# Pooling products in three reduced-precision passes, with the differences split into high and low parts by ScalarE and VectorE

## The chip, the core and the metric

The kernel runs on one core of a Trainium2 chip. The metric is the device time of one execution in microseconds (us), lower is better. The five engines of a core run side by side, each taking the instructions of its own queue in order: TensorE (PE: matmuls; its weight loads are PEld), VectorE (DVE), ScalarE (ACT), GpSimd (POOL) and SyncE (SP, here the issuer of most DMAs). They wait for each other through semaphores.

## What is computed

One decoder layer over a sequence of 1024 tokens of width 1024, all in float32. A normed input is projected to 1536 columns: 512 for a pooling mixer, 512 for a gated recurrence (RG-LRU), 512 for its gate. The mixers' outputs are normed, projected back and added, and a SwiGLU feed-forward layer follows. The change is in the pooling mixer:

```python
def pool_mixer(u, pool_w, pool_scale):
    for g, w in enumerate(POOL_WINDOWS):            # (2, 4, 8, 16)
        ug = uf[..., g * POOL_GROUP:(g + 1) * POOL_GROUP]
        cs = jnp.cumsum(ug, axis=1)
        lag = jnp.pad(cs[:, :S - w], ((0, 0), (w, 0), (0, 0)))
        mean = (cs - lag) / jnp.minimum(pos, float(w))
        outs.append(mean - ug)
    d = jnp.stack(outs, axis=2)
    y = jnp.einsum('bsgc,gcd->bsgd', d, pool_w.astype(jnp.float32)).reshape(B, S, POOL_WIDTH)
    return (y * pool_scale.astype(jnp.float32)).astype(u.dtype)
```

Each of the four groups has 128 channels and a 128x128 matrix, so a product here is 128x128 by 128x1024.

## The kernel before

Everything is held transposed, channels on the 128 partitions and tokens along the free dimension. Nearly all matmuls are done in three passes: an operand is split into a high part, rounded to the reduced-precision type fp32r by a ScalarE cast, and a low part, the rest, by a VectorE or GpSimd subtraction; then low x high, high x low and high x high are added up in one PSUM bank (`three_pass`, and `product` in the feed-forward layer). The gate matmuls of the recurrence (`gates`) and the pooling products (`pool_product`) are the exceptions: plain float32 matmuls on unsplit tiles.

The input projection runs over twelve blocks of 128 columns, c = 0 to 11. Blocks 0 to 3 feed the recurrence, 4 to 7 (from `POOL0` = 4) the pooling, 8 to 11 (from `GATE0` = 8) the gate. A block has two halves of 512 tokens, each 24 matmuls (8 row tiles x 3 passes). On every engine a loop over c writes out the order of the work by hand:
- TensorE: first half of block c; the gate matmuls of recurrence block c - 2 (c up to 5) or the pooling product p = c - 6 (c from 6 to 9, p = 0 to 3); second half; the other gate matmuls of c - 1. A product has two matmuls, one for each half of the tokens, into two banks that it shares with the gates.
- VectorE: in the round of block c it scales the first half out of PSUM (`first_half`, L1135), then does the recurrence c - 2 (`recur`, up to c = 5; ends with a scan, L1212), takes the result of product c - 6 out of PSUM with its gains (`pool_output`, L1240), makes the differences of the pooling block c - 4 (`window_mean`: p + 1 window sums L1224, the difference L1229, a repair of the first 16 tokens), and then the low part of the weights of block c + 2 (`split_w`, L1276), which TensorE needs in order to begin that block.
- ScalarE: in the round of block c it evacuates or activates the first half, takes the square root of the recurrence (L759), squares the product c - 6 (`pool_squares`, L771), evacuates the second half (L732, or the gelu L735), casts the weights of block c + 2 (`split_w`, L647) and does two sigmoids (L745).
- GpSimd adds the squares of products 1 to 3 to those of product 0 (L600).

The differences of product p lie in `xc[p % 2]`; `window_mean` may write them again once product p - 2 is done. `d_ok` counts the differences, `poolmm_ok` the halves of the products, `u_ok` and `u_first_ok` the evacuated halves, `w_lo_ok` the low parts of weights. In the last phase the blocks of the down weights (`dn`) have one semaphore each, for which ScalarE's `split_dn` and VectorE's `down_sum` wait.

Of the kernel before, what the change touches and what calls it, by code (L numbers as in the profile page):

```python
# [24 lines left out]
F32R = mybir.dt.float32r  # L25
ALU = mybir.AluOpType
ACT = mybir.ActivationFunctionType

P = 128
# [3 lines left out]
def hymba_pool_rglru_block(nc, x, ln1_g, w_in, pool_w, pool_scale, conv_w, conv_b, w_a, b_a, w_i, b_i,  # L33
                           lam, gn_pool_g, gn_lru_g, w_out, ln2_g, w_gate, w_up, w_down, lnf_g, out):
    S, D = x.shape[1], x.shape[2]
# [4 lines left out]
    GT = GW // P  # L40
# [4 lines left out]
    NP = FT // 2  # L45
# [8 lines left out]
    POOL0, GATE0 = GT, 2 * GT  # L54
# [10 lines left out]
    with ExitStack() as ctx:  # L65
# [3 lines left out]
        def at(name, kib, shape, dt=F32):  # L69
            return nc.alloc_sbuf_tensor_at(name, shape, dt, offset=BASE + int(kib * KIB))  # L70
# [9 lines left out]
        xc = [at(f"xc{s}", 120 + 4 * s, [P, S]) for s in range(2)]  # L80
# [21 lines left out]
        y1_lo = at("y1_lo", 168.25, [P, GT, S], F32R)  # L102
        sq_scr = at("sq_scr", 196.25, [P, 512])

        xs2 = [at(f"xs2_{s}", 116 - 4 * s, [P, D]) for s in range(2)]


# [79 lines left out]
        def sem(name):  # L187
            return ctx.enter_context(nc.semaphore(name))
# [7 lines left out]
        gate_1_in = sem("gate_1_in")  # L196
        hid_out = sem("hid_out")
        h_raw_in = [sem(f"h_raw_in{s}") for s in range(STEPS)]
        dn_in = {bk: sem(f"dn_in{bk[0]}_{bk[1]}") for bk in DN_ORDER}
        stored = sem("stored")  # L200

        consts = sem("consts")
# [15 lines left out]
        rb_ok = sem("rb_ok")  # L218
# [3 lines left out]
        sq_a_ok, sq_half_ok = sem("sq_a_ok"), sem("sq_half_ok")  # L222
        fin_act_ok = sem("fin_act_ok")
        psq_ok = sem("psq_ok")
        lsq_ok = sem("lsq_ok")
        ys_hi_ok, wo_hi_ok = sem("ys_hi_ok"), sem("wo_hi_ok")
        raw_ok = sem("raw_ok")
# [62 lines left out]
        def f32(ap):  # L290
            return ap.bitcast(F32)
# [4 lines left out]
        def half(i):  # L296
            return slice(i * HALF, (i + 1) * HALF)
# [344 lines left out]
        def _(act):  # L642
# [118 lines left out]
            def pool_squares(p):  # L761

                for i in range(2):
# [4 lines left out]
                    if p >= 2 and i == 0:  # L768
# [2 lines left out]
                    act.activation(dst[:, half(i)], pg[w % 2][:], ACT.Square, scale=v("pool_scale", p))\  # L771
                        .then_inc(psq_ok, 1)

            def lru_squares(g):
                act.wait_ge(lmul_ok, g + 1)
                if g >= 1:
                    act.wait_ge(ssum_ok, GT - 1 + g - 1)
                dst = ssum[1] if g == 0 else rg
                act.activation(dst[:], y[1][:, g, :], ACT.Square).then_inc(lsq_ok, 1)
# [37 lines left out]
            for c in range(2, NC_IN):  # L817
                if 0 <= c - 2 < GT:
                    sigmoids(c - 2, 1)
                    decay(c - 2)  # L820
                evacuate(c, 0)
                if 0 <= c - 2 < GT:
                    root(c - 2)
                if 0 <= c - POOL0 - 2 < GT:
                    pool_squares(c - POOL0 - 2)
                if c == NC_IN - 1:
                    y_hi_part(0)
                    y_hi_part(1)
                    group_sqrt(0)
                evacuate(c, 1)  # L830
                if c + 2 < NC_IN:
                    split_w(c + 2)
                if 0 <= c - 1 < GT:
                    sigmoids(c - 1, 0)
                if c - 1 >= GATE0:
                    lru_squares(c - 1 - GATE0)
                if c == NC_IN - 2:
                    split_wo(0)
# [138 lines left out]
            def split_dn(s):  # L977
                i, k = s // NP, s % NP
                pr = PRODUCTS[i]
                if pr in ("M1", "M2", "M3"):  # L980
                    act.wait_ge(dn_in[D_BLOCK[pr], k], 16)
                else:
                    act.wait_ge(dsum_ok, dsum_count(DSUM_OF[pr], k))
                if s < STEPS:
                    act.wait_ge(ent_ok, done(entry(FT - 1, "M6")) if s < EARLY else NE)
                act.copy(d_hi[s % STEPS][:], dn[D_BLOCK[pr], k][:]).then_inc(d_hi_ok, 1)
# [87 lines left out]
        def _(dve):  # L1074
# [139 lines left out]
            def window_mean(p):  # L1214
# [18 lines left out]
                                              op0=ALU.max, op1=ALU.mult))  # L1233
                dve.tensor_tensor(d[:, 0:PAD], dfix[:], src[:, PAD:2 * PAD], ALU.subtract).then_inc(d_ok, 1)

            def pool_output(p):
                for i in range(2):
                    w = 2 * p + i
                    dve.wait_ge(psq_ok, w + 1)
                    dve.tensor_scalar(y[0][:, p, half(i)], pg[w % 2][:], v("pool_scale", p), v("gn_pool", p),  # L1240
                                      ALU.mult, ALU.mult).then_inc(pool_y, 1)
# [36 lines left out]
            for c in range(NC_IN):  # L1278
                if c >= 2:
                    first_half(c)  # L1280
                if 0 <= c - 2 < GT:
                    recur(c - 2)
                if 0 <= c - POOL0 - 2 < GT:
                    pool_output(c - POOL0 - 2)
                if c < POOL0:
                    convolve(c)
                    if c == 0:
                        softplus()
                elif c < GATE0:
                    window_mean(c - POOL0)  # L1290
                else:
                    if c == NC_IN - 1:
                        group_variance(0)
                        group_rsqrt(0)
                    gate_lru(c - GATE0)
                    if c > GATE0:
                        lru_gain(c - GATE0 - 1)
                if c + 2 < NC_IN:
                    split_w(c + 2)
                if c == NC_IN - 2:  # L1300
                    split_wo(0)
# [194 lines left out]
            def down_sum(name, k):  # L1496
                b11, b12, b21, b22 = (dn[b, k][:] for b in ("11", "12", "21", "22"))
                if name == "T3":
                    dve.wait_ge(dn_in["22", k], 16)
                    dve.wait_ge(dn_in["12", k], 16)  # L1500
                    dve.tensor_tensor(b12, b22, b12, ALU.subtract).then_inc(dsum_ok, 1)
                if name == "T2":
                    dve.wait_ge(d_lo_ok, k + 1)
                    dve.wait_ge(dsum_ok, dsum_count("T3", k))
                    dve.tensor_tensor(b11, b12, b11, ALU.add).then_inc(dsum_ok, 1)
                if name == "T1":
                    dve.wait_ge(d_lo_ok, 3 * NP + k + 1)
                    dve.wait_ge(dsum_ok, dsum_count("T2", k))
                    dve.tensor_tensor(b12, b22, b11, ALU.subtract).then_inc(dsum_ok, 1)
                if name == "T4":  # L1510
                    dve.wait_ge(dn_in["21", k], 16)
                    dve.wait_ge(dsum_ok, dsum_count("T1", k))
                    dve.tensor_tensor(b11, b21, b11, ALU.subtract).then_inc(dsum_ok, 1)
# [87 lines left out]
        def _(pe):  # L1601
# [53 lines left out]
                        .then_inc(gates_ok, 1)  # L1655

            def pool_product(p):
                pe.wait_ge(d_ok, p + 1)
                for i in range(2):
                    w = 2 * p + i  # L1660
                    if p == 0:
                        pe.wait_ge(gate_evac, 4 * GT - 1 + i)
                    else:
                        pe.wait_ge(pool_y, w - 1)
                    pe.matmul(pg[w % 2][:], pool_ws[:, p], xc[p % 2][:, half(i)], start=True, stop=True)\  # L1665
                        .then_inc(poolmm_ok, 1)

            def group_sums(g):

# [206 lines left out]
```

## Time and profile before

| | before |
|---|---|
| median of three runs | 922.02 us (921.94 to 923.41) |
| the profiled execution: time, span | 922.02 us, 920.2 us |
| busy share of TensorE, VectorE, ScalarE, GpSimd | 97%, 66%, 42%, 30% |
| chain of work that ended last | TensorE 95%, VectorE 3%, DMA 1% |
| pooling products (L1665) | 16 records of 592 ns |
| a load of one block of input weights, 512 KB | 3.7 us from issue to landing |

The span is the time from the first to the last instruction of the profiled execution; the time of a run has some 1.8 us more around it. A float32 matmul leaves two records in the trace, a pass of a split one leaves one. Matmuls are pipelined: a record of 0.39 us overlaps the next, so the cost of one is the distance between the starts. The granted clock tells at which of its two levels (2.4 GHz: 1.00; 1.2 GHz: 0.5) TensorE ran. In a timeline row stand the start, the duration, the engine and line, the operation, what it writes and reads, its shape and the count of merged instructions, and in brackets how long the engine had idled and for whom.

### The profile page before, as it was taken

The numbers are of one execution on the slowest core, as the hardware profiler recorded it, in microseconds if no ns is written. First come the engines' busy times: TensorE is split into PE (matmuls) and PEld (weight loads), VectorE is DVE, ScalarE is ACT, GpSimd is POOL, SyncE is SP. The second block draws the span as 40 slices with busy tenths as digits, with TensorE's granted clock in tenths as the row PEclk, the third lists the DMA queues.
The fourth block names the chain that finished last, engine by engine and source line by source line (L and its number), as shares of the span: only waits on it lengthen the run. The fifth ranks groups of instructions, "written<-read, shape, count | busy, mean of one in ns | idle before, by whom it ended". The sixth has DMA issues, their size and how long they took to land.

```text
span 920.2 us, 10969 instructions
## 1 busy us (share of the span) xinstructions
PE 895.2 (97%) x3955; PEld 731.2 (79%) x3955; DVE 606.0 (66%) x836; ACT 388.4 (42%) x645; POOL 277.6 (30%) x213
## 2 busy tenths in 40 slices
PE   5989999999999999999999999999999999999996
PEld 4757777888888788888888888888888888888885
DVE  5568885455568866565665656646566985687766
ACT  5668723433466433322323233232334343445455
POOL 3000012255043755446455545555551000000000
PEclk9999999999999999999999999999999999999998
DMA  9010110204002132233322423324238943332324
GB/s 320 1 47 23 46 46 24 92 1 159 24 1 70 46 125 81 92 126 92 126 95 78 149 70 125 109 71 154 72 111 307 405 145 103 92 103 93 98 86 183
DMA packets 93790, 96.43 MB, mean 105 GB/s; under 512 B 5628, under 2 KB 63528, under 8 KB 93736
## 3 DMA queue, kind: packets, MB, share of 16 engines
q1 hardware_dynamic: 83224, 76.32, 24.5%
q10 hardware_dynamic: 10512, 19.40, 6.8%
q8 instruction: 32, 0.52, 0.2%
q14 instruction: 22, 0.18, 0.1%
HBM read 71.33 MB, written 24.38 MB: 104 GB/s over the span
## 4 chain that ended last, share of the span: by engine, by line
PE 95%; DVE 3%; DMA 1%; issue 1%; ACT 0%; POOL 0%; DVEq 0%; ACTq 0%
PE bank L1734 23%; PE bank L1736 23%; PE bank L1735 23%; PE bank L1606 8%; PE bank L1608 7%; PE bank L1607 7%; PE bank L1623 1%; PE bank L1654 1%; PE bank L1665 1%; DVE nT_lo L1127 1%; DMA g_row<-in_ln_g 1%; DVE xc L1118 0%; PE bank L1672 0%; DVE xc L1193 0%; DVE xc L1120 0%
## 5 line engine op out<-in xcount | busy, mean ns | idle before, releaser
L618 POOL TENSOR_TENSOR r_lo<-gu_raw,r_hi 128x512 fp32r<-128x512 f32 x84 | 116.4, 1385 | 68.1 <-ACT r_hi L862 68.0
L618 POOL TENSOR_TENSOR r_lo<-wsum_S,r_hi 128x512 fp32r<-128x512 f32 x63 | 98.7, 1567 | 125.7 <-ACT r_hi L862 125.7
L1734 PE MATMUL bank<-T_hi,r_lo 128*128 128x512 f32 x336 | 130.9, 390 | 0.9 <-DVE u L1461 0.9
L1736 PE MATMUL bank<-T_hi,r_hi 128*128 128x512 f32 x336 | 130.7, 389 | 0.0
L1735 PE MATMUL bank<-T_lo,r_hi 128*128 128x512 f32 x336 | 130.7, 389 | 0.0
L1734 PE MATMUL bank<-d_hi,h_lo 128*128 128x512 f32 x308 | 119.8, 389 | 0.0
L1735 PE MATMUL bank<-d_lo,h_hi 128*128 128x512 f32 x308 | 119.8, 389 | 0.0
L1736 PE MATMUL bank<-d_hi,h_hi 128*128 128x512 f32 x308 | 119.8, 389 | 0.0
L862 ACT CAST r_hi<-gu_raw 128x512 fp32r<-128x512 f32 x84 | 52.2, 621 | 131.4 <-PE bank L1736 131.4
L1734 PE MATMUL bank<-nT_hi,r_lo 128*128 128x512 f32 x252 | 98.1, 389 | 0.0
L1735 PE MATMUL bank<-nT_lo,r_hi 128*128 128x512 f32 x252 | 98.0, 389 | 0.0
L1736 PE MATMUL bank<-nT_hi,r_hi 128*128 128x512 f32 x252 | 98.0, 389 | 0.0
L975 ACT CAST h_hi<-h_raw 128x512 fp32r<-128x512 f32 x76 | 47.2, 622 | 102.5 <-PE bank L1736 98.0
L1606 PE MATMUL bank<-nT_hi,w_lo 128*128 128x512 f32 x192 | 81.2, 423 | 5.1 <-DVE nT_lo L1127 2.6
L1439 DVE TENSOR_TENSOR h_lo<-h_raw,h_hi 128x512 fp32r<-128x512 f32 x76 | 52.5, 691 | 47.8 <-ACT h_hi L975 47.8
L1608 PE MATMUL bank<-nT_hi,w_hi 128*128 128x512 f32 x192 | 75.5, 393 | 0.0
L1607 PE MATMUL bank<-nT_lo,w_hi 128*128 128x512 f32 x192 | 75.5, 393 | 0.0
L1734 PEld LDWEIGHTS bank<-T_hi,r_lo 128*128 128x128 f32 x336 | 63.1, 188 | 14.6 <-POOL r_lo L618 1.3
L1736 PEld LDWEIGHTS bank<-T_hi,r_hi 128*128 128x128 f32 x336 | 63.1, 188 | 13.2
L1735 PEld LDWEIGHTS bank<-T_lo,r_hi 128*128 128x128 f32 x336 | 63.1, 188 | 13.1
L1734 PEld LDWEIGHTS bank<-d_hi,h_lo 128*128 128x128 f32 x308 | 57.8, 188 | 12.1
L1735 PEld LDWEIGHTS bank<-d_lo,h_hi 128*128 128x128 f32 x308 | 57.8, 188 | 12.0
(208 smaller groups left out, 1627.1 us busy)
## 6 DMA issues: line engine op xcount, KB each, us to landing
h_raw<-hid_ops ACTq DMA_DIRECT2D x72, 256.0 KB, 2.6
gu_raw<-in_w_ffn_gate SPq DMA_DIRECT2D x22, 512.0 KB, 3.7
gu_raw<-in_w_ffn_up SPq DMA_DIRECT2D x22, 512.0 KB, 4.7
hid_ops<-hid SPq DMA_DIRECT2D x44, 256.0 KB, 2.2
dn<-in_w_ffn_down SPq DMA_DIRECT2D x44, 256.0 KB, 10.8
hid_ops<-hsum_S SPq DMA_DIRECT2D x33, 256.0 KB, 2.5
w_raw<-in_w_in SPq DMA_DIRECT2D x12, 512.0 KB, 3.7
h<-in_x SPq DMA_DIRECT2D x8, 512.0 KB, 7.6
```

Of the source, the lines that this page charges most:

```text
L618: pool.tensor_tensor(lo_of(n)[:], a_block(f, name), f32(hi_of(n)[:]), ALU.subtract)\
L862: act.copy(hi_of(n)[:], a_block(f, name)).then_inc(r_hi_ok, 1)
L975: act.copy(h_hi[s % STEPS][:], h_source(s)[:]).then_inc(h_hi_ok, 1)
L1127: dve.tensor_tensor(nT_lo[dst], pt_of(n)[b][:].rearrange("p (k n) -> p k n", k=4), f32(nT_hi[dst]), ALU.subtract).then_inc(n_lo_ok, 1)
L1439: dve.tensor_tensor(h_lo[s % STEPS][:], h_source(s)[:], f32(h_hi[s % STEPS][:]), ALU.subtract)\
L1606: pe.matmul(bank, s_lo, m_hi, start=(k == 0), stop=False)
L1607: pe.matmul(bank, s_hi, m_lo, start=False, stop=False)
L1608: ins = pe.matmul(bank, s_hi, m_hi, start=False, stop=(k == n - 1))
L1623: ins = pe.transpose(pt_of(n)[b][:, cols(k)], xs[n % 2][:, cols(4 * b + k)], ident[:])
L1734: pe.matmul(bank, s_lo, m_hi, start=(opens and j == 0), stop=False, skip_group_check=True)
L1735: pe.matmul(bank, s_hi, m_lo, start=False, stop=False, skip_group_check=True)
L1736: ins = pe.matmul(bank, s_hi, m_hi, start=False, stop=(closes and j == n - 1), skip_group_check=True)
```

## The change

Each pooling product becomes six fp32r matmuls instead of two float32 ones. The weights are split once: ScalarE casts all four matrices at the end of the round of block 4 (`pool_weights_hi`), VectorE subtracts in the round of block 5 (`pool_weights_lo`, in place). The differences of product p are split in the round of block p + 5: ScalarE casts them behind the squares and ahead of the second half's evacuation (`pool_hi`), VectorE subtracts in place ahead of the next block's window sums (`pool_lo`). The product waits for the low parts. The high parts lie in space that is free at that time, which adds two waits to ScalarE (for the last scan, and for product p - 2). In the last phase the blocks "12" and "22" of the down weights share a semaphore, since both are loaded in turn.

```diff
+        pw_hi, pw_lo = at("pw_hi", 200.5, [P, GT, P], F32R), at("pw_lo", 188.25, [P, GT, P], F32R)
+        pd_hi = [at(f"pd_hi{s}", (164.25, 148.25)[s], [P, S], F32R) for s in range(2)]
+        pd_lo = [at(f"pd_lo{s}", 120 + 4 * s, [P, S], F32R) for s in range(2)]
...
-        dn_in = {bk: sem(f"dn_in{bk[0]}_{bk[1]}") for bk in DN_ORDER}
+        dn_in = {bk: sem(f"dn_in{bk[0]}_{bk[1]}") for bk in DN_ORDER if bk[0] != "12"}
+        for k in range(NP):
+            dn_in["12", k] = dn_in["22", k]
...
+            def pool_weights_hi():
+                act.wait_ge(small_in, 16 * 5)
+                act.wait_ge(rb_ok, 1)
+                act.copy(pw_hi[:], pool_ws[:]).then_inc(pw_hi_ok, 1)
+            def pool_hi(p):
+                act.wait_ge(d_ok, p + 1)
+                if p == 1:
+                    act.wait_ge(scan_ok, GT)
+                if p >= 2:
+                    act.wait_ge(poolmm_ok, 2 * (p - 1))
+                act.copy(pd_hi[p % 2][:], xc[p % 2][:]).then_inc(pd_hi_ok, 1)
...
                 if 0 <= c - POOL0 - 2 < GT:
                     pool_squares(c - POOL0 - 2)
+                if 0 <= c - POOL0 - 1 < GT:
+                    pool_hi(c - POOL0 - 1)
...
                 evacuate(c, 1)
+                if c == POOL0:
+                    pool_weights_hi()
...
-                    act.wait_ge(dn_in[D_BLOCK[pr], k], 16)
+                    act.wait_ge(dn_in[D_BLOCK[pr], k], 32 if pr == "M3" else 16)
...
+            def pool_weights_lo():
+                dve.wait_ge(pw_hi_ok, 1)
+                dve.tensor_tensor(pw_lo[:], pool_ws[:], f32(pw_hi[:]), ALU.subtract).then_inc(pw_lo_ok, 1)
+            def pool_lo(p):
+                dve.wait_ge(pd_hi_ok, p + 1)
+                dve.tensor_tensor(pd_lo[p % 2][:], xc[p % 2][:], f32(pd_hi[p % 2][:]), ALU.subtract).then_inc(pd_lo_ok, 1)
...
                 if 0 <= c - POOL0 - 2 < GT:
                     pool_output(c - POOL0 - 2)
+                if c == POOL0 + 1:
+                    pool_weights_lo()
+                if 0 <= c - POOL0 - 1 < GT:
+                    pool_lo(c - POOL0 - 1)
                 if c < POOL0:
                     convolve(c)
...
-                    dve.wait_ge(dn_in["22", k], 16)
-                    dve.wait_ge(dn_in["12", k], 16)
+                    dve.wait_ge(dn_in["22", k], 32)
...
             def pool_product(p):
-                pe.wait_ge(d_ok, p + 1)
+                pe.wait_ge(pw_lo_ok, 1)
+                pe.wait_ge(pd_lo_ok, p + 1)
                 for i in range(2):
                     w = 2 * p + i
...
-                    pe.matmul(pg[w % 2][:], pool_ws[:, p], xc[p % 2][:, half(i)], start=True, stop=True)\
-                        .then_inc(poolmm_ok, 1)
+                    three_pass(pg[w % 2][:], [(pw_hi[:, p], pw_lo[:, p], pd_hi[p % 2][:, half(i)],
+                                               pd_lo[p % 2][:, half(i)])]).then_inc(poolmm_ok, 1)
```

## Rows read from the trace of the kernel before

**Rows 1.** Windows view, 100 to 180 us: busy time (instructions) of each engine, clock, DMA
```profile
100.00:180.00 80.00, 80.00 (x343) 62.97 (x342) 54.50 (x56) 29.41 (x39) 10.17 (x5) 1.00 0.14 43
```

**Rows 2.** Waits of TensorE: total us, times, longest
```profile
PE bank L1606 <- DVE w_lo L1276: 2.5, 1, 2.5
...
PE bank L1606 <- POOL y_lo L625: 0.5, 1, 0.5
```

**Rows 3.** Timeline of TensorE, 101 to 153 us: start, us, instruction, [idle before]
```profile
101.85 1.88 PE L1654 MATMUL bank<-xc,gate_w 128*128 128x512 f32 x4
...
109.05 0.39 PE L1606 MATMUL bank<-nT_hi,w_lo 128*128 128x512 f32 x1
...
114.49 1.88 PE L1665 MATMUL bank<-xc,pool_ws 128*128 128x512 f32 x4
...
127.14 1.88 PE L1665 MATMUL bank<-xc,pool_ws 128*128 128x512 f32 x4
...
152.43 1.88 PE L1665 MATMUL bank<-xc,pool_ws 128*128 128x512 f32 x4
```

**Rows 4.** Timeline of VectorE, 115 to 124 us
```profile
115.23 1.20 DVE L1224 TENSOR_TENSOR sumA<-ub 128x1024 f32<-128x1024 f32 x1
...
119.28 1.22 DVE L1276 TENSOR_TENSOR w_lo<-w_raw,w_hi 128x1024 fp32r<-128x1024 f32 x1
...
121.99 1.53 DVE L1240 TENSOR_SCALAR y<-bank,vec 128x512 f32<-128x512 f32 x2 [0.88 <-ACT ig L771]
123.43 1.21 DVE L1224 TENSOR_TENSOR sumA<-ub 128x1024 f32<-128x1024 f32 x1
```

**Rows 5.** One line's instructions: VectorE split of 128x512, ns min/median/max
```profile
L1439 DVE TENSOR_TENSOR h_lo<-h_raw,h_hi x76: 682/692/695, 698.8 to 900.2; 128x512 fp32r<-128x512 f32 x76
```

**Rows 6.** Instruction groups by line: ScalarE cast of 128x1024, 80 to 330 us
```profile
L647 ACT CAST w_hi<-w_raw 128x1024 fp32r<-128x1024 f32 x7 | 7.4, 1052 | 0.0
```

**Rows 7.** Timeline of ScalarE, 99 to 123 us
```profile
99.97 0.68 ACT L745 ACTIVATE ig<-bank,vec 128x512 f32<-128x512 f32 x1
...
110.38 0.57 ACT L732 COPY ub<-bank 128x512 f32<-128x512 f32 x1
...
121.26 1.27 ACT L771 ACTIVATE ig<-bank,vec 128x512 f32<-128x512 f32 x2 [9.37 <-DVE ub L1135]
122.42 0.59 ACT L732 COPY ub<-bank 128x512 f32<-128x512 f32 x1
```

**Rows 8.** Timeline of VectorE, 128 to 143 us
```profile
128.76 1.22 DVE L1276 TENSOR_TENSOR w_lo<-w_raw,w_hi 128x1024 fp32r<-128x1024 f32 x1
...
135.23 1.23 DVE L1224 TENSOR_TENSOR sumA<-ub 128x1024 f32<-128x1024 f32 x1 [2.23 <-ACT ub L732]
...
141.83 1.22 DVE L1276 TENSOR_TENSOR w_lo<-w_raw,w_hi 128x1024 fp32r<-128x1024 f32 x1
142.97 0.68 DVE L1135 TENSOR_TENSOR ub<-bank,rb 128x512 f32<-128x512 f32 x1
```

**Rows 9.** Timeline of ScalarE, 143 to 146 us
```profile
143.75 1.28 ACT L735 ACT_TABLE_LOAD   x1 [7.67 <-DVE ub L1135]
...
145.58 1.25 ACT L771 ACTIVATE rg<-bank,vec 128x512 f32<-128x512 f32 x2
```

**Rows 10.** Timeline, GpSimd's second addition of squares
```profile
146.91 2.41 POOL L600 TENSOR_TENSOR ig<-ig,rg 128x1024 f32<-128x1024 f32 x1 [12.42 <-ACT rg L771]
```

**Rows 11.** Timeline of VectorE, beside that addition
```profile
147.82 2.58 DVE L1246 TENSOR_TENSOR y<-y,ub 128x1024 f32<-128x1024 f32 x1
```

**Rows 12.** Timeline of VectorE, the low weights that it waited for
```profile
51.56 1.22 DVE L1276 TENSOR_TENSOR w_lo<-w_raw,w_hi 128x1024 fp32r<-128x1024 f32 x1
```

**Rows 13.** Timeline of TensorE, its one wait for low weights
```profile
52.83 0.50 PE L1606 MATMUL bank<-nT_hi,w_lo 128*128 128x512 f32 x1 [2.48 <-DVE w_lo L1276]
```

**Rows 14.** Windows view, two early stretches; the clock is the number behind GpSimd's
```profile
14.00:21.00 7.00, 4.41 (x14) 3.37 (x13) 5.05 (x13) 6.50 (x12) 3.75 (x2) 0.76 1.10 367
...
48.00:53.00 5.00, 2.15 (x5) 0.85 (x6) 4.45 (x21) 4.57 (x6) 0.00 (x0) 1.00 0.01 2
```

More of the change, by code:

```diff
@@ L224, in hymba_pool_rglru_block @@
         psq_ok = sem("psq_ok")
+        pw_hi_ok, pw_lo_ok, pd_hi_ok, pd_lo_ok = (sem(n) for n in ("pw_hi_ok", "pw_lo_ok", "pd_hi_ok", "pd_lo_ok"))
         lsq_ok = sem("lsq_ok")
```

## The prediction

> **What bounds the kernel now.** I read the windows view first. From 100 to 180 us, the stretch that holds all four pooling products, TensorE is busy for the whole of it at a granted clock of 1.00 (its 2.4 GHz level), VectorE for 54.5 us of 80, ScalarE for 29.4 [rows 1]. Then TensorE's waits: it waits once for a low part of weights, for 2.5 us before this stretch, and once behind it, 0.5 us, for a low part that GpSimd makes [rows 2]. So TensorE sets the time. What it no longer has to do is won one for one, and what it must newly wait for is lost one for one. Both VectorE and ScalarE are half idle on average, but an average doesn't say whether a part is ready at the moment when TensorE asks; for that the timelines have to be laid side by side.
>
> **What the products cost on TensorE.** I number the column blocks c = 0 to 11; blocks 4 to 7 are the pooling ones, and product p (0 to 3) stands inside block p + 6, between its two halves. Each half of a block is 24 matmuls. The first half of block 6 starts at 109.05 and product 0 at 114.49, so 24 matmuls take 5.44 us, 0.2267 each [rows 3]. From product 0 to product 1 are 12.65 us (product 3 lies two such periods further on, to 0.01); less 48 x 0.2267 = 10.88, a full-precision product of four records costs 1.77 us [rows 3]. In three passes it is 2 halves x 3 = 6 matmuls of the kind around it: 6 x 0.2267 = 1.36. The gain is 0.41 each and 4 x 0.41 = 1.64 in all. The period between products falls from 12.65 to 12.24.
>
> **What it costs elsewhere: product 0.** Until now product 0 needed only the differences, and these are made in VectorE's round of block 4. The low half of them is made in the round of block 5, and there VectorE runs the last recurrence first: what follows its scan, today the first window sum, starts at 115.23 [rows 4]. That alone is 0.74 us after TensorE reaches product 0. Now two splits come ahead of the window sum. The weights' low part is 128x512 elements, 0.69 us [rows 5], less 0.08 of overlap with the next instruction (two back-to-back instructions start 1.14 apart where the first takes 1.22 [rows 8]), so 0.61; the other split can start at 115.84. The differences' low part is 128x1024, as the split of weights beside it, 1.22 us [rows 4]: done at 117.06. ScalarE's high part is ready: its round of block 5 is free at 110.38 [rows 7], a cast takes 1.05 [rows 6], so about 111.4. TensorE starts a matmul 0.05 after a low part lands (51.56 + 1.22 to 52.83), and the first one after a wait lasts 0.50 instead of 0.39 [rows 3, 12, 13]. Product 0 therefore starts at 117.11 instead of 114.49, and the stall is 2.62 + 0.11 = 2.73 us. Nothing covers it, since TensorE takes its queue in order and the second half of block 6 is behind it.
>
> **The other edits, followed down the chain.** TensorE's products now stand at 117.22 (with the 0.11), and then every 12.24: 129.46, 141.70, 153.94. VectorE's chain is what must keep up.
> - Block 6. The two splits move VectorE's work by 0.61 + 1.14 = 1.75. The weights' low part of block 7, today 119.28 to 120.50 [rows 4], ends at 122.25; TensorE wants it at 117.22 + 1.36 + 5.44 = 124.02. Covered, but only because of the stall: without one it would be wanted at 121.29. The first half's scaling runs 1.14 behind the start of the split, from 122.17 to 122.85; ScalarE's squares follow 0.16 later, at 123.01 (121.10 to 121.26 today), with 1.16 to its next instruction [rows 7], and the cast runs from 124.17 to 125.22. VectorE's low part of product 1 runs from 125.30 to 126.52 and the window sums start at 126.44, against 123.43 [rows 4]: a shift of 3.01. Product 1 asks at 129.46, covered by 2.9.
> - Block 7. With the shift of 3.01 the low weights of block 8 end at 132.99 [rows 8]; wanted at 136.26. By the same steps the scaling ends at 133.59, the squares of product 1 run from 133.75 to 135.02, and GpSimd adds them to the sum from 135.10 for 2.4 us. ScalarE's cast ends at 135.96, so VectorE's low part of product 2 comes while GpSimd adds. The trace has this meeting once: GpSimd's addition from 146.91 to 149.32 and a VectorE product of two tiles from 147.82, which lasts 2.58 instead of 1.23 and ends 1.08 after GpSimd [rows 10, 11]. I take that: the low part ends at 137.50 + 1.08 = 138.58, and the window sums start at 138.50 against 135.23, a shift of 3.27 [rows 8]. The 2.23 us that VectorE idled there are used up. Product 2 asks at 141.70, covered by 3.1. The low weights of block 9 end at 146.32; wanted at 148.50.
> - Block 8. The scaling ends at 142.97 + 3.27 + 0.68 = 146.92 [rows 8]. From there a table load, the gelu and the squares take ScalarE to 146.92 + 0.10 + 3.08 = 150.10 (143.75 to 146.83 today [rows 9]), and the last cast to about 151.05. GpSimd adds from 150.18 to 152.58, so the last low part ends at 153.66, with 0.05 for TensorE 153.71. Product 3 asks at 153.94: covered by 0.23 only. Behind it come a gate product and the low weights of block 10, 1.2 each, done by about 156.1 and wanted at 153.94 + 1.36 + 5.44 = 160.74.
> - Queued behind ScalarE's casts are the second half's evacuation and the next weights' high part. In block 5 the evacuation moves from 110.38 to about 111.4 [rows 7], read by the window sums after 117; in the others the low part, which waits for the same cast, is later anyway. The load of block 9's weights on SP's queue waits for the low part at 122.25, 1.75 later than today, takes 3.7 us (the table) and is read by ScalarE after 135.
> - The weights' high part, a ScalarE cast of half the size and so at most 1.05 [rows 6], delays the sigmoids whose last one ends at 100.65 [rows 7] and which release the gate matmuls that start at 101.85 [rows 3]. It is hidden, as I put it at about half of 1.05; if it cost all of it, still within 1.2. The one semaphore for two blocks of the down weights counts the same two transfers; its waits end where the later one ended. Nothing.
>
> A rule of the page "SBUF — State Buffer" of the Trainium skill ("Who interferes with whom") says the same of the block: a VectorE instruction with two SBUF inputs and a GpSimd one that reads SBUF exclude each other for the whole instruction, whoever came first. The trace agrees (2.58 against 1.23). If they only shared, each of the two low parts would last about 1.3 us less and product 3 would have some 2.9 to spare; the sum stays, since product 0 is stalled before GpSimd adds anything.
>
> **The sum.** -1.64 + 2.73 = +1.09 us. The profiled execution has a span of 920.2 and a time of 922.02, which is also the median; 1.8 lie around the span. All that follows block 9 hangs on TensorE (the 0.5 for GpSimd's low part too: its chain starts at the last block's gelu), so the 1.09 arrive at the end: 923.1 us. The sum is robust downward: if product 0 were late by less, TensorE would reach block 7 and product 3 earlier and wait there, for 122.25 and 153.71, which are VectorE's times. By VectorE's chain alone the three last steps would still give 153.71 + 0.11 - 152.43 - 0.41 = +0.98. Upward there is no such floor: each delay of VectorE's chain beyond 0.23 us arrives at product 3.
>
> **Rivals.**
> 1. Slower: the last high part comes late. In block 8 ScalarE goes from gelu to squares to the cast and back to gelu. If the cast between them cost one more table load, 1.28 [rows 9], ahead of it, the last low part would be ready at 154.99 and product 3 would stall for 1.05 + 0.11: 923.1 + 1.16 = 924.3, slower by 0.24%. It decides from 0.23 us on, and passes the bound from 0.9. Against it: today a cast of weights stands between such gelus, and VectorE's longer idle times have no load in them. For it: the cover is a quarter of a microsecond at the end of a chain of some twenty instructions. 0.19.
> 2. No stall: product 0 finds its low part ready and the gain stands alone, 922.02 - 1.64 = 920.4. For this the split would have to be over by 114.49, but the recurrence ahead of it isn't. 0.04. A gain of more than 0.2% has no cause in the rows beyond this one.
> 3. Three passes bring nothing, because switching from and to full precision costs less than I count or weight loads come in between: +2.73, 924.8. Against it stand hundreds of such matmuls at 0.2267 with loads beside them. 0.03.
> 4. The pause costs TensorE its clock. Today it stood for 2.48 us and the granted clock stayed 1.00 [rows 13, 14]; early on, with TensorE busy for 4.4 of 7 us, it was 0.76 over them, so 0.24 x 7 = 1.7 us lost at most [rows 14]. 923.1 + 1.7 = 924.8. 0.04.
> Of this the page "TensorE: Matmul & The Clock Gate" ("What's actually happening") says that the array is throttled by default and activity releases it; the trace shows one pause of the same length without a drop, so I go by the trace.
>
> **How the numbers follow.** Forecast 0.70, with a range of its own of 922.4 to 923.8 (0.7 either way for the twenty-odd durations and the spread of the three runs of before, 921.94 to 923.41). A measurement of this kernel tells about 0.2%, 1.84 us, from no change: 920.18 and 923.86. Slower: rivals 1, 3 and 4, 0.26, of which some fall under the bound: 0.24. Faster: 0.03, from rival 2. Same: 0.73. The range reaches up to rival 1 and down past my own range: 921.6 to 924.6.
>
> **What would show it.** In the changed kernel TensorE waits for the differences' low part once, for about 2.6 us, at product 0, and for nothing at block 7; products are some 12.24 apart; VectorE's low parts 2 and 3 last about 2.5 us instead of 1.22; product 3 follows within 0.3 us of its low part. The forecast is wrong if product 0 doesn't wait, if product 3 waits for over 0.5, or if TensorE's clock falls after product 0.

## Result and the profile after

| | before | after |
|---|---|---|
| median | 922.1 us (17 runs, 921.94 to 924.76) | 924.64 us (17 runs, 923.08 to 926.16) |
| ratio after / before | | 1.0021, 95% interval 1.0014 to 1.0028 |
| the profiled execution: span | 920.2 us | 924.3 us |
| TensorE, VectorE, ScalarE, GpSimd busy, us | 895.2, 606.0, 388.4, 277.6 | 897.7, 612.7, 392.6, 276.9 |

The changed kernel is slower by about 2 us where 1.09 was forecast. The measured median lies 0.04 above the top of the range that was given (924.6); by the ratio, 922.02 x 1.0021 = 924.0 lies inside, and above the forecast's own range (923.8). It is on the far side of the prediction's 0.2% line, if only just: "slower" had 0.24, "same" 0.73. The seventeen runs don't scatter about one value. Four lie at 923.08 to 923.13, six at 924.49 to 924.81, and seven at 925.06 to 926.16. The first group is the forecast (922.02 + 1.09 = 923.11) and the question is what the others pay.

The profiled execution is one of the longest (926.14 us). Its timeline of TensorE at product 0 (start, us, instruction, idle before) answers to the product in [rows 3]:

```profile
115.63 0.39 PE L1647 MATMUL bank<-nT_hi,w_hi 128*128 128x512 f32 x1
118.51 0.56 PE L1645 MATMUL bank<-pd_hi,pw_lo 128*128 128x512 f32 x1 [2.49 <-issue]
118.87 0.63 PE L1646 MATMUL bank<-pd_lo,pw_hi 128*128 128x512 f32 x1
119.29 0.63 PE L1647 MATMUL bank<-pd_hi,pw_hi 128*128 128x512 f32 x1
...
121.43 0.63 PE L1646 MATMUL bank<-nT_lo,w_hi 128*128 128x512 f32 x1
121.85 0.54 PE L1647 MATMUL bank<-nT_hi,w_hi 128*128 128x512 f32 x1
122.23 0.40 PE L1645 MATMUL bank<-nT_hi,w_lo 128*128 128x512 f32 x1
```

The pause is there, 2.49 us idle (the view names "issue" because the wait stands ahead of the product and not on the matmul). Behind it the matmuls are 0.427 us apart instead of 0.2267, until 122.23: nine of them and the start take 3.72 us where 9 x 0.2267 + 0.11 = 2.15 would do. That is 1.57 us on top of the pause. The windows view (us, then busy time of TensorE, its weight loads, VectorE, ScalarE, GpSimd; the number behind GpSimd's is the granted clock), first after, then before:

```profile
14.00:21.00 7.00, 4.42 (x15) 3.40 (x14) 5.05 (x13) 6.54 (x12) 3.77 (x2) 0.76 1.09 363
54.00:58.00 4.00, 4.00 (x13) 3.10 (x12) 3.47 (x3) 0.00 (x0) 0.00 (x0) 0.59 0.40 118
118.00:122.00 4.00, 3.49 (x9) 2.74 (x10) 3.93 (x4) 0.00 (x0) 0.00 (x0) 0.59 0.00 0
```

```profile
54.00:58.00 4.00, 4.00 (x20) 3.28 (x19) 3.71 (x3) 0.00 (x0) 0.00 (x0) 1.00 0.45 130
118.00:122.00 4.00, 4.00 (x19) 3.29 (x19) 3.05 (x6) 0.74 (x2) 0.00 (x0) 1.00 0.03 8
```

Apart from the start, where both kernels show 0.76, TensorE's clock fell to its 1.2 GHz level twice in this execution of the changed kernel: at product 0, and near 54 us, behind the older pause for the low weights of block 2, in code that the change doesn't touch. In the profiled execution of before it fell at neither, though the older pause was there [rows 13].

### The profile page after: what moved, and what is told of

It reads as the page before. It is cut to its first block, busy times and chain, and to the rows that moved or that the text cites. A ratio compares the mean times of both kernels' runs of the same rounds, so it can differ in the third digit from the quotient of the medians.

```text
span 924.3 us, 10988 instructions
## 1 busy us (share of the span) xinstructions
PE 897.7 (97%) x3963; PEld 735.5 (80%) x3963; DVE 612.7 (66%) x841; ACT 392.6 (42%) x650; POOL 276.9 (30%) x213
## 4 chain that ended last, share of the span: by engine, by line
PE 89%; DVE 6%; issue 2%; ACT 2%; DMA 1%; POOL 0%; ACTq 0%; DVEq 0%
PE bank L1774 23%; PE bank L1776 23%; PE bank L1775 23%; PE bank L1645 6%; PE bank L1647 6%; PE bank L1646 6%; PE bank L1662 1%; DVE xc L1221 1%; DVE nT_lo L1155 1%; DMA g_row<-in_ln_g 1%; DVE t2b L1236 1%; DVE w_lo L1312 1%; ACT t2b L768 0%; DVE xc L1146 0%; ACT L768 0%
## 5 line engine op out<-in xcount | busy, mean ns | idle before, releaser
L1776 PEld LDWEIGHTS bank<-d_hi,h_hi 128*128 128x128 f32 x308 | 57.8, 188 | 12.1
```

The source lines that it names most:

```text
L1776: ins = pe.matmul(bank, s_hi, m_hi, start=False, stop=(closes and j == n - 1), skip_group_check=True)
```

## The experiments

Theory A: the sum of the prediction holds (+1.09), and the rest is the clock that falls in the pause at product 0 in many executions (rival 4, which had 0.04). Theory B: the rest is somewhere else, in product 3 waiting for its low part (rival 1) or in another part of the change. Each kernel below ran in five rounds beside the kernel before; "mean" below is against the mean of all 108 runs of the kernel before that stood beside the changed kernel or the experiments, 922.83 (lowest 921.85).

**The changed kernel again.**

> The changed kernel unaltered, beside the next three on one chip. All theories: its runs lie at 923.1 or above, median about 924.6. Theory A: none lies between 922.2 and 923.0, and those above 923.1 are 1.2 to 3.2 us higher, by one or two falls of the clock (start, 50 us, product 0).

Ratio 1.0022 (1.0013 to 1.0031), median 924.6; two of 11 runs at 923.13 and 923.18, none below. This time the profiled execution is one of the lowest (923.18, span 921.4), with the clock at 1.00 from 54 to 58 and from 118 to 122. It shows the change without any fall. TensorE at the four products, and then VectorE's splits and low weights:

```profile
117.13 0.47 PE L1645 MATMUL bank<-pd_hi,pw_lo 128*128 128x512 f32 x1 [2.48 <-issue]
...
129.49 0.39 PE L1645 MATMUL bank<-pd_hi,pw_lo 128*128 128x512 f32 x1
...
141.73 0.39 PE L1645 MATMUL bank<-pd_hi,pw_lo 128*128 128x512 f32 x1
...
153.97 0.39 PE L1645 MATMUL bank<-pd_hi,pw_lo 128*128 128x512 f32 x1
```

```profile
115.23 0.67 DVE L1266 TENSOR_TENSOR pw_lo<-pool_ws,pw_hi 128x512 fp32r<-128x512 f32 x1
115.81 1.22 DVE L1270 TENSOR_TENSOR pd_lo<-xc,pd_hi 128x1024 fp32r<-128x1024 f32 x1
...
121.02 1.22 DVE L1312 TENSOR_TENSOR w_lo<-w_raw,w_hi 128x1024 fp32r<-128x1024 f32 x1
...
125.24 1.22 DVE L1270 TENSOR_TENSOR pd_lo<-xc,pd_hi 128x1024 fp32r<-128x1024 f32 x1
...
135.94 2.60 DVE L1270 TENSOR_TENSOR pd_lo<-xc,pd_hi 128x1024 fp32r<-128x1024 f32 x1
...
145.05 1.22 DVE L1312 TENSOR_TENSOR w_lo<-w_raw,w_hi 128x1024 fp32r<-128x1024 f32 x1
...
151.02 2.61 DVE L1270 TENSOR_TENSOR pd_lo<-xc,pd_hi 128x1024 fp32r<-128x1024 f32 x1
```

The prediction had the products at 117.11, 129.46, 141.70 and 153.94. Product 3's low part ends at 151.02 + 2.61 = 153.63; with 0.05 for the start it is covered by 0.29 (0.23 was said). Low parts 2 and 3 last 2.6 us because GpSimd adds squares from 135.06 and 150.13:

```profile
135.06 2.40 POOL L609 TENSOR_TENSOR ig<-ig,rg 128x1024 f32<-128x1024 f32 x1 [116.38 <-ACT rg L780]
150.13 2.42 POOL L609 TENSOR_TENSOR ig<-ig,rg 128x1024 f32<-128x1024 f32 x1 [12.67 <-ACT rg L780]
```

135.06 + 2.40 = 137.46, and the low part ends 1.08 later, as in [rows 10, 11]. So rival 1 did not happen.

This profile also prices the change without the start of the kernel, which differs from execution to execution. I measure from the first matmul of block 2, behind the older pause, to the last store that is issued ("SPq" is SP's queue); first the changed kernel's two rows, then the last one of before, whose first is in [rows 13]:

```profile
52.85 0.50 PE L1645 MATMUL bank<-nT_hi,w_lo 128*128 128x512 f32 x1 [2.47 <-DVE w_lo L1312]
...
918.72 0.43 SPq L570 DMA_DIRECT2D out_dram<-h  x1
```

```profile
917.58 0.43 SPq L561 DMA_DIRECT2D out_dram<-h  x1
```

918.72 - 52.85 = 865.87 against 917.58 - 52.83 = 864.75: +1.12 us, where the sum was +1.09. And it accounts for the execution of 926.14 us. That one takes 1.64 us more from block 2's first matmul to product 0 (65.92 against 64.28, the fall near 54 us) and 1.57 more from product 0 to the last store (803.16 against 801.59, the fall at product 0). Nothing is left for a third cause.

**The pause filled.** TensorE does idle matmuls (their result is read by nobody) while it waits at product 0:

```diff
             def pool_product(p):
+                if p == 0:
+                    for _ in range(10):
+                        pe.matmul(pt[0][:], nT_hi[:, 0, 0:P], nT_hi[:, 1, half(0)], start=True, stop=True)
                 pe.wait_ge(pw_lo_ok, 1)
```

> The changed kernel with ten idle matmuls (of normed input tiles, into a bank that nobody reads) ahead of product 0's wait: 10 x 0.2267 = 2.27 us of the 2.6 us for which TensorE stands still there. Theory A (the pause lets TensorE's clock fall to its 1.2 GHz level, which costs about 1.4 us on top of the wait): the clock stays at 1.00 through 118 to 122 us, product 0 starts when it did, and the median falls from about 924.6 to 923.1 to 923.5, what is left over 923.1 coming from the older pause near 50 us. Theory B (the excess over the forecast comes from product 3 waiting for its low part, or from the last phase): nothing changes, about 924.6.

```profile
117.05 2.43 PE L1699 MATMUL bank<-nT_hi 128*128 128x512 f32 x10
119.70 0.47 PE L1645 MATMUL bank<-pd_hi,pw_lo 128*128 128x512 f32 x1 [0.22 <-issue]
```

```profile
54.00:58.00 4.00, 4.00 (x11) 3.21 (x12) 3.93 (x4) 0.00 (x0) 0.00 (x0) 0.62 0.46 131
118.00:122.00 4.00, 3.78 (x17) 2.85 (x16) 3.96 (x4) 0.00 (x0) 0.00 (x0) 1.00 0.00 0
```

Median 923.57, ratio 1.0013 (1.0004 to 1.0022), mean +1.13 where the changed kernel's 28 runs have +1.97. Five of 11 runs lie at 923.06 to 923.21. The product starts as late as before (VectorE's chain stands where it stood, the execution being 2.6 us late by falls at the start and at 54 us), but the clock behind the pause is 1.00. The median is 0.07 above the expected range. The means differ by 1.97 - 1.13 = 0.84 us, which would be 1.57 in about every second execution. This figure is rough: single runs of a kernel differ by up to 3 us, the two ratios' intervals overlap, and on 11 and 28 runs I estimate the 0.84 to about 0.7 either way. That the mean comes within 0.04 of the sum, 1.09, is luck, since it holds falls elsewhere too, as the mean of before does. A second estimate comes from the lowest group: 6 of the changed kernel's 28 runs lie in it (up to 923.2) and 44 of the 108 of before (up to 922.1). If the falls are independent of each other, the one at product 0 spares about half of the executions. The profiled run, 925.73, owes its length to falls elsewhere; that the other one above 925.7 does too is inferred.

**Three-pass products alone**, of tiles that are there already. The splits are left out on ScalarE and VectorE, and the products are of other data, so this kernel doesn't compute the layer; it only times the products:

```diff
             def pool_product(p):
-                pe.wait_ge(pw_lo_ok, 1)
-                pe.wait_ge(pd_lo_ok, p + 1)
+                pe.wait_ge(d_ok, p + 1)
...
-                    three_pass(pg[w % 2][:], [(pw_hi[:, p], pw_lo[:, p], pd_hi[p % 2][:, half(i)],
-                                               pd_lo[p % 2][:, half(i)])]).then_inc(poolmm_ok, 1)
+                    three_pass(pg[w % 2][:], [(nT_hi[:, p, 0:P], nT_hi[:, p, 0:P], nT_hi[:, p, half(i)],
+                                               nT_lo[:, p, half(i)])]).then_inc(poolmm_ok, 1)
```

> Three-pass products alone: six fp32r matmuls for each product, but of normed input tiles that are there already, with no splits and with the wait for the differences as before the change. The splits of weights and differences are left out and the products are of other data. Both theories: no pause at product 0, the products 12.24 us apart, 0.41 x 4 = 1.64 us less than the kernel before, 920.4 (ratio 0.9982). A rival that the three passes save nothing: 922.0.

Lowest runs 920.28 to 920.32 (five of 11), against 921.85 to 922.07 before; mean -1.56, ratio 0.9984 (0.9975 to 0.9993). The first two products in the profile:

```profile
117.02 0.39 PE L1637 MATMUL bank<-nT_hi 128*128 128x512 f32 x1
...
129.26 0.39 PE L1637 MATMUL bank<-nT_hi 128*128 128x512 f32 x1
```

They are 12.24 us apart, and there is no pause. The gain term of 4 x 0.41 is right; rival 3 falls.

**Splits and waits alone**, the products in full precision and the low parts in space of their own: once as it is, and once with idle matmuls in both pauses (the ten at product 0, nine ahead of block 2).

```diff
...
-        pd_lo = [at(f"pd_lo{s}", 120 + 4 * s, [P, S], F32R) for s in range(2)]
+        pd_lo = [at(f"pd_lo{p}", 164.25 if p == 3 else 160.25, [P, S], F32R) for p in range(4)]
...
-                    three_pass(pg[w % 2][:], [(pw_hi[:, p], pw_lo[:, p], pd_hi[p % 2][:, half(i)],
-                                               pd_lo[p % 2][:, half(i)])]).then_inc(poolmm_ok, 1)
+                    pe.matmul(pg[w % 2][:], pool_ws[:, p], xc[p % 2][:, half(i)], start=True, stop=True)\
+                        .then_inc(poolmm_ok, 1)
```

> The splits and the waits alone: everything of the change but the products, which stay in full precision and read the unsplit tiles; the low parts are written aside. A pause of 2.6 us at product 0 and nothing won: by the sum +2.73, 924.8 without a fall of the clock. Theory A: with the fall, some 1.4 more in most runs, median about 926.2. Theory B: 924.8.

> The splits and waits with full-precision products, with the idle matmuls in both pauses. The pause at product 0 priced by itself without the clock: 922.0 + 2.73 = 924.8, or 923.7 where the start-up runs without its fall; median 924.8, against 926.9 without the idle matmuls. If splits and waits cost something besides the pause and the clock, it stays above 925.5.

Without the idle matmuls: median 926.93 of only five runs, mean +4.03; none at 924.8. With them: median 924.76, mean +2.12, five of ten runs at 924.4 to 924.8, four at 925.5 to 925.7 and one at 923.73. From block 2's first matmul to the last store the profiled execution with them takes 867.45 us, +2.70 against before: that is the 2.73 of the prediction. The means of the two kernels differ by 1.9 us, and all five runs without idle matmuls are longer than all ten with them; since both pauses are filled at once, this doesn't say which of the two falls it saves. The profile without them shows that a pause alone decides nothing. The clock had fallen at the start and near 54 us; at product 0 TensorE stood idle as long as in the changed kernel, and the clock stayed:

```profile
116.70 0.39 PE L1649 MATMUL bank<-nT_hi,w_hi 128*128 128x512 f32 x1
119.57 1.96 PE L1707 MATMUL bank<-xc,pool_ws 128*128 128x512 f32 x4 [2.49 <-issue]
...
120.96 0.79 PE L1647 MATMUL bank<-nT_hi,w_lo 128*128 128x512 f32 x1
```

```profile
118.00:122.00 4.00, 2.43 (x7) 1.42 (x8) 3.93 (x5) 0.00 (x0) 0.00 (x0) 1.00 0.00 0
```

(From the product to the next matmul of a block are 1.39 us; in the kernel before, without a pause, 1.32, from 114.49 to 115.81.) The same 2.49 us of pause cost 1.57 us in one execution and nothing in another.

**The kernel before, with its own pause filled.**

```diff
                 u = position(c, i)
+                if i == 0 and c == 2:
+                    for _ in range(9):
+                        pe.matmul(pt[0][:], nT_hi[:, 0, 0:P], nT_hi[:, 1, half(0)], start=True, stop=True)
                 if i == 0:
                     pe.wait_ge(w_lo_ok, c + 1)
```

> The kernel before with nine idle matmuls ahead of its wait for the low weights of block 2 (2.5 us near 50 us). Theory A, applied to the older pause: the runs of the kernel before that take 923.4 instead of 922.0 are those in which the clock falls there; with the idle matmuls all runs take 922.0, and the highest stays under 922.6. Theory B: the spread of 1.4 us stays.

Ten of 11 runs lie between 920.92 and 922.04, the last at 923.13, against a highest of 924.70 and a median of 923.1 for the kernel before beside it. Ratio 0.9989 (0.998 to 0.9998). So the spread of the kernel before is for the most part the same thing: a pause in which the clock falls or not. "All runs at 922.0" was wrong in both directions.

There is a third place, the start of the kernel. In the windows view from 14 to 21 us the granted clock was 0.76 to 0.78 in nine of the fourteen profiles, 0.63 to 0.65 in four, and 1.00 in one (a run of 920.47 of a kernel below). One of the four (a run of 921.45 of the last kernel below, whose median is 920.35), and the one with 1.00, with its next 7 us:

```profile
14.00:21.00 7.00, 4.41 (x13) 3.33 (x12) 5.05 (x13) 6.51 (x12) 3.77 (x2) 0.63 1.10 368
```

```profile
14.00:21.00 7.00, 4.41 (x21) 3.53 (x20) 5.05 (x13) 6.53 (x12) 3.78 (x2) 1.00 1.10 365
21.00:28.00 7.00, 5.13 (x27) 4.28 (x26) 5.11 (x11) 3.38 (x8) 0.00 (x0) 0.83 0.21 63
```

In the second the low stretch isn't missing; it comes later. What each start costs shows at the first matmul of block 2: 52.48 us with the late stretch, 52.59 to 52.92 with 0.76 to 0.78, and 53.91 to 54.03 in the four with 0.63 to 0.65. So the longer low stretch costs about 1.1 us, which fits a run at 923.1. Runs 1.1 us *below* the usual lowest ones, as 920.9 here, are in no profile. Their mean granted clock on record is 0.998 against 0.994 to 0.997 of this kernel's others, so it is the clock; but they appear only with idle matmuls ahead of block 2 (8 of the 53 runs of the five kernels that have them, none of the 108 of before), and why that is stays open.

**Both pauses filled in the changed kernel.**

> The changed kernel with idle matmuls in both pauses: nine ahead of block 2, ten ahead of product 0. Theory A (the sum +1.09 stands, and the rest of the excess is TensorE's clock falling in pauses): the clock stays at 1.00 in both places in the profile, nothing lies above 924.3, and the median is 923.1 or, where the start-up too runs without its fall (1.1 less, as in the lowest runs with the matmuls ahead of block 2), 922.0 to 923.1. A rest of theory B (an excess that has nothing to do with pauses): median over 924.

Ratio 1.0008 (1.0000 to 1.0017), median 923.18, the profiled execution 923.09 with the clock at 1.00 in both places. Five of 11 runs at 923.00 to 923.18, one at 922.20, but five at 924.0 to 924.45, one of which is above the 924.3 that was said. They lie 1.1 above the group at 923.1, as a longer low stretch at the start would put them. Their mean granted clock is 0.993 to 0.995, that of the group at 923.1 0.996 to 0.997, so it is the clock; no profile of one of them was taken, so where it fell stays open. In the profiled execution block 2's first matmul to the last store takes 865.85 us, +1.10 against 864.75, both in before and in before with its own pause filled. The runs of these two kernels with filled pauses differ by 1.26 in the median and 1.73 in the mean: the profile gives the sum, and the mean holds more falls than the pauses that were filled.

**Product 0 left in full precision**, products 1 to 3 as in the change (their waits and the weights' splits are counted without product 0):

```diff
-                if 0 <= c - POOL0 - 1 < GT:
+                if 1 <= c - POOL0 - 1 < GT:
                     pool_hi(c - POOL0 - 1)
...
-                if 0 <= c - POOL0 - 1 < GT:
+                if 1 <= c - POOL0 - 1 < GT:
                     pool_lo(c - POOL0 - 1)
...
+                    if p == 0:
+                        pe.matmul(pg[w % 2][:], pool_ws[:, 0], xc[0][:, half(i)], start=True, stop=True)\
+                            .then_inc(poolmm_ok, 1)
+                        continue
```

> The changed kernel with product 0 left in full precision on the unsplit tiles; products 1 to 3 in three passes. No split and no wait for product 0. From the rows of before: three gains of 0.41; product 3 would be asked for at 152.43 - 2 x 0.41 = 151.61, while VectorE's low part is ready at about 152.5, 1.1 to 1.2 earlier than in the change because one split fewer stands ahead of it: a pause of 0.9 + 0.11. Sum -1.23 + 1.0 = -0.2, lowest runs 921.8. Theory A: a pause of 0.9 does not bring the clock down, so the distribution is that of the kernel before, shifted by -0.2 (ratio 0.9998). If VectorE's chain doesn't matter at product 3: -1.2, 920.8.

Lowest runs 921.72 and 921.75, 0.3 below 922.02 where 0.2 was said; mean -0.03, ratio 0.9997 (0.9988 to 1.0006). Product 3 now waits, and its distance to product 2 is 13.09 instead of 12.24, a pause of 0.85 (0.9 + 0.11 was said):

```profile
141.10 0.39 PE L1645 MATMUL bank<-pd_hi,pw_lo 128*128 128x512 f32 x1
...
154.19 0.47 PE L1645 MATMUL bank<-pd_hi,pw_lo 128*128 128x512 f32 x1 [0.69 <-issue]
```

This is the kind of floor of which the prediction spoke: without the pause at product 0 VectorE's chain holds up product 3 instead, and most of the gain of three products, 0.85 of 1.23, goes there. Its 11 runs span 921.7 to 924.4, as the kernel before's span 921.9 to 924.65: this shorter pause brings no new group of runs.

**The splits moved, so that no product waits.** Product 0 in full precision; then, in a second kernel, all four in three passes. The calls stand at their new places only.

```diff
                     decay(c - 2)
+                if 1 <= c - POOL0 - 1 < GT:
+                    pool_hi(c - POOL0 - 1)
                 evacuate(c, 0)
...
                 if c >= 2:
                     first_half(c)
+                if c == POOL0 + 1:
+                    pool_weights_lo()
+                if 1 <= c - POOL0 - 1 < GT:
+                    pool_lo(c - POOL0 - 1)
```

> Product 0 in full precision as before, products 1 to 3 in three passes, and the splits moved: ScalarE's cast at the top of its round, where it idles for 6 to 10 us waiting for VectorE's first scaling; VectorE's low part right behind that scaling, where it overlaps the squares and ends before GpSimd's addition starts; the weights' low part ahead of the last recurrence. No low part is late and none meets GpSimd: each lasts 1.22. All theories: -3 x 0.41 = -1.23, lowest runs 920.8, ratio 0.9987. If the moved splits delay anything (a second half's evacuation, the low weights of blocks 8 and 9), up to 0.5 of it is lost.

> The same with the nine idle matmuls ahead of the wait for the low weights of block 2. Theory A: same lowest runs (920.8) but fewer above them, as in the kernel before with these matmuls; median 920.8, ratio to the kernel before about 0.998.

The second kernel begins `pool_hi` with product 0 and has besides:

```diff
+                if j == GT - 1:
+                    pool_lo(0)
                 dve.wait_ge(sqrt_ok, j + 1)
...
+                    if c == POOL0 + 1:
+                        split_w(c + 2)
                     window_mean(c - POOL0)
...
-                if c + 2 < NC_IN:
+                if c + 2 < NC_IN and c != POOL0 + 1:
                     split_w(c + 2)
```

> All four products in three passes, none late: the high part of product 0 is cast between ScalarE's exponential and its square root, its low part taken in the 2.5 us in which VectorE waits for that root, the weights' low part ahead of the recurrence, the low weights of block 7 ahead of the window sums of the second pooling block; products 1 to 3 as in the kernel with the splits moved. The last recurrence ends 1.0 us later. -4 x 0.41 = -1.64: lowest runs 920.4, ratio to the kernel before 0.998. Rival: the recurrence's 1.0 us comes out at the low weights of block 7 or 8, and it is no faster than the kernel with product 0 in full precision, 920.8.

> The same with the nine idle matmuls ahead of block 2. Lowest runs 919.3 (start-up without its fall) or 920.4, median 920.2 to 920.4, ratio to the kernel before 0.9975: the fastest of all kernels here.

| kernel | median, us | lowest | ratio to before (95%) |
|---|---|---|---|
| product 0 full, splits moved | 920.86 | 920.81 | 0.9986 (0.9976 to 0.9995) |
| the same, idle matmuls ahead of block 2 | 920.68 | 919.75 | 0.9979 (0.9970 to 0.9988) |
| all four split, splits moved | 920.46 | 920.24 | 0.9985 (0.9976 to 0.9994) |
| the same, idle matmuls ahead of block 2 | 920.35 | 919.38 | 0.9974 (0.9965 to 0.9984) |

All beat both kernels. Seven of the first one's 11 runs lie at 920.81 to 920.87, where 922.02 - 1.23 = 920.79 was the sum. With all four split the low part of product 0 lies in VectorE's idle time and the low parts of the later ones last 1.22 us again, since they come ahead of GpSimd's addition. In the timeline of VectorE of that kernel the first of them waits 0.5 us for ScalarE's cast and is still done 4 us before the product:

```profile
108.87 1.23 DVE L1272 TENSOR_TENSOR pd_lo<-xc,pd_hi 128x1024 fp32r<-128x1024 f32 x1 [0.47 <-ACT pd_hi L796]
...
132.00 1.21 DVE L1272 TENSOR_TENSOR pd_lo<-xc,pd_hi 128x1024 fp32r<-128x1024 f32 x1
...
144.19 1.22 DVE L1272 TENSOR_TENSOR pd_lo<-xc,pd_hi 128x1024 fp32r<-128x1024 f32 x1
```

```profile
114.29 0.39 PE L1649 MATMUL bank<-pd_hi,pw_lo 128*128 128x512 f32 x1
```

Whether the fourth product's 0.41 is really there can't be told from the ratios (their intervals overlap). From the profiles it can. The table has, from the first matmul of block 2 to the last store, every profiled execution whose clock stayed at 1.00 in between, up to the last matmul:

| kernel | us | against before |
|---|---|---|
| before; before, pause filled | 864.75; 864.75 | 0 |
| changed; changed, both pauses filled | 865.87; 865.85 | +1.12; +1.10 |
| splits and waits alone, both filled | 867.45 | +2.70 |
| product 0 full, splits moved; with idle matmuls | 863.56; 863.51 | -1.19; -1.24 |
| all four split, splits moved; with idle matmuls | 863.11; 863.09 | -1.64; -1.66 |

The fourth product brings 0.42 to 0.45. The terms of the prediction's sum come out to 0.04 us in single executions, where the ratios' intervals are over 1 us wide.

The profiles can be counted for the falls too. Ahead of block 2 TensorE stood for 2.47 or 2.48 us in nine of them, and the clock fell behind it in five; at product 0 it stood for 2.48 or 2.49 in three, and it fell in one. In the eight cases in which one of these pauses was filled it never fell.

## Why the prediction was right and where it was wrong

- **The gain on TensorE** (0.41 each, 1.64): right; the products alone have a period of 12.24, and all four without a pause give -1.64 from block 2 to the end.
- **The pause at product 0** (2.73): right, at its place and by its cause, the low part behind the last recurrence on VectorE. 117.13 for 117.11; splits and waits alone, with the pauses filled, +2.70 for +2.73.
- **The chain behind it**: right to 0.1 us over forty microseconds, with the cover of 0.29 at product 3 and the two low parts held up by GpSimd. A floor of this kind showed itself when product 0 no longer waited.
- **Rival 1's price** was a slip in the prediction. One more table load, 1.28, would have put the end of the last cast (150.99 in the profile) at 152.27, still under GpSimd's addition, which ends at 152.55 and beside which the low part ends 1.08 later in any case. By the prediction's own reading product 3 would have waited for next to nothing, and not for 1.16. So the 0.19 for it, most of "slower", stood on a price that its own rows don't give.
- **The hidden parts** (the weights' cast, the evacuations, the shared semaphore): nothing of them appears; the gate matmuls start at 101.84 for 101.85, and the whole is +1.12.
- **The clock** (rival 4): this is the step that failed. The prediction said that TensorE had stood for 2.48 us in the kernel before with the clock at 1.00, and gave a fall 0.04, "so I go by the trace". The trace was one execution. In five of the nine profiles with that same pause, in code that the change doesn't touch, the clock did fall; the spread of the three runs (921.94 to 923.41) already held the sign of it, and the prediction took it for noise in its own range. By a sign that the prediction named itself ("if TensorE's clock falls after product 0") it was wrong in such executions. The price was fair (1.7 at most; 1.57 measured), the chance was not: about one execution in two, as far as the groups of runs tell. The rule of the Trainium skill ("TensorE: Matmul & The Clock Gate", "What's actually happening"), that the array is throttled by default and that activity releases it, was cited and set aside for one row. The profiles agree with it: the clock fell in or behind stretches in which TensorE stood, in six of the twelve pauses of 2.5 us, and in none of the eight that were filled.
- **The side of the line**: 1.12 + half of 1.57 = 1.9 us is 0.21%. With a chance of a half for rival 4 the prediction would have put its middle at 923.9 and "slower" near a half. That the ratio lies inside the stated range is partly luck: its top was set by rival 1, which did not happen and whose price was the slip above.

## What to carry to other kernels

When a new operand is made one round later than the old one, look at what its engine does first in that round: the average load says nothing, the start time of one instruction says it all. A pause of TensorE has two prices, its length and the clock behind it; the second one depends on the execution, so read it from the spread of several runs and not from one profile, and give a new pause of the length seen here, 2.5 us, a real chance of it. To price a change in single profiles, measure between two instructions with the clock at 1.00 in between. The splits cost nothing here where they lay in an engine's idle time and ahead of the GpSimd addition beside which a low part lasts 2.6 us instead of 1.22; the same splits and products were worth +1.12 us in one order and -1.64 in another.

## What was not expected of the hardware

- A pause of 2.49 us of TensorE was followed by 1.57 us lost at the 1.2 GHz level in one execution and by nothing in another. Filling all but 0.2 us of it with matmuls that nobody needs kept the clock at 1.00 in each of the three profiles that have them; what this takes off the mean is 0.84 us, known to about 0.7.
- The kernel before pays for its own older pause: nine idle matmuls there make it faster, 0.9989 (0.998 to 0.9998), though they add work.
- The start differs for the same instructions: the granted clock from 14 to 21 us was 0.76 to 0.78 in nine profiles, 0.63 to 0.65 in four and 1.00 in one, where the low stretch came behind 25 us. The long one cost 1.1 us, the late one 0.1 to 0.4 less than the usual one.
